# Attention: row maxima of the coming block over 16 key tiles instead of 17, VectorE's additions of probabilities one a step

## The reference, cut to what matters

```python
def one_block(qblk):
    s = jnp.einsum('bqkgd,blkd->bkgql', qblk, k).astype(jnp.float32) * scale
    p = jax.nn.softmax(s, axis=-1).astype(v.dtype)
    return jnp.einsum('bkgql,blkd->bqkgd', p, v)
```

## Time and profile before

| what | us |
|---|---|
| median of 3 runs | 3497.44 (3494.97 to 3501.01) |
| the profiled execution: its time | 3497.05 |
| the profiled execution: its span (first to last instruction) | 3495.4 |
| attention, from the first block to the last values | about 586 to 1818 |

### The profile page before, as it was taken

One profiled execution on the slowest core, in us unless ns is written; L12 is line 12 of the kernel. 1 busy time (PEld: TensorE's weight loads), 2 busy tenths in 40 slices (PEclk: granted clock), 3 DMA queues, 4 the chain that ended last, 5 costly groups with the idle time before them and its releaser, 6 DMA issues. The chain is left out here.

```text
span 3495.4 us, 39397 instructions
## 1 busy us (share of the span) xinstructions
PE 3276.0 (94%) x14481; PEld 2416.4 (69%) x14481; DVE 2103.9 (60%) x3047; ACT 1014.2 (29%) x1405; POOL 1272.1 (36%) x710
## 2 busy tenths in 40 slices
PE   6999766999999999999979979999999999999996
PEld 3888753655556565655647758888888888888885
DVE  3444435686777767677756655555555556665557
ACT  3232231343434434343433232222111111111111
POOL 1233201666666566555551122222222223332221
PEclk8999986999999999999999989999999999999998
DMA  5123296122321232232027861111111612221111
GB/s 228 55 87 90 74 344 176 43 63 52 99 58 52 53 88 57 52 75 49 16 64 256 290 234 66 48 48 48 48 48 48 247 60 72 72 72 55 48 47 48
DMA packets 221243, 325.91 MB, mean 93 GB/s; under 512 B 27152, under 2 KB 153488, under 8 KB 215824
## 3 DMA queue, kind: packets, MB, share of 16 engines
q1 hardware_dynamic: 201040, 295.14, 28.0%
q10 hardware_dynamic: 18944, 25.17, 2.2%
q0 software_dynamic: 1152, 4.19, 0.3%
HBM read 228.70 MB, written 95.75 MB: 93 GB/s over the span
## 5 line engine op out<-in xcount | busy, mean ns | idle before, releaser
L976 DVE TENSOR_REDUCE a_mpart<-a_mx 128x1 f32<-128x512 f32 (+1 forms) x960 | 592.8, 636 | 322.9 <-PE a_mx L1066 312.5
L921 POOL TENSOR_TENSOR a_acc_p<-a_acc_p,a_pf 128x1024 f32<-128x1024 f32 x240 | 581.1, 2421 | 233.3 <-ACT a_pf L957 211.6
L957 ACT ACTIVATE a_pf<-a_sc 128x1024 f32<-128x1024 f32 x432 | 441.7, 1025 | 468.7 <-PE a_sc L1091 467.8
L1623 DVE TENSOR_TENSOR f_yacc<-f_two,f_yacc 128x512 f32<-128x512 f32 x480 | 328.4, 690 | 257.7 <-PE f_two L1718 257.6
L1718 PE MATMUL f_two<-f_w_hi,f_h_hi 128*128 128x512 f32 x1024 | 398.4, 389 | 1.6 <-DVE f_h_lo L1636 1.6
L1718 PE MATMUL f_two<-f_w_hi,f_h_lo 128*128 128x512 f32 x1024 | 398.4, 389 | 0.0
L1718 PE MATMUL f_two<-f_w_lo,f_h_hi 128*128 128x512 f32 x1024 | 398.3, 389 | 0.0
L1104 PE MATMUL a_o<-a_pf,a_v 128*64 128x512 f32 x1728 | 390.5, 601 | 0.0
L1561 POOL TENSOR_TENSOR f_w_lo<-w_rows,f_w_hi 128x1024 fp32r<-128x1024 f32 x64 | 158.5, 2481 | 546.9 <-ACT f_w_hi L1520 546.7
L1633 DVE TENSOR_TENSOR f_relu<-f_relu 128x512 f32<-128x512 f32 x128 | 192.7, 1506 | 242.5 <-ACT f_relu L1530 242.5
L1104 PEld LDWEIGHTS a_o<-a_pf,a_v 128*64 128x64 f32 x1728 | 120.8, 138 | 231.0 <-issue 221.2
(11 more groups left out here) (266 smaller groups left out, 6074.5 us busy)
## 6 DMA issues: line engine op xcount, KB each, us to landing
w_rows<-in_w SPq DMA_DIRECT2D x128, 512.0 KB, 3.9
a_wa<-in_w_ada SPq DMA_DIRECT2D x6, 2048.0 KB, 9.8
ada_w<-in_w_ada SPq DMA_DIRECT2D x8, 1024.0 KB, 8.0
xt<-in_x_t SPq DMA_DIRECT2D x16, 512.0 KB, 3.6
o_m_hi<-s_mix ACTq DMA_DIRECT2D x8, 1024.0 KB, 7.1
o_m_lo<-s_mix ACTq DMA_DIRECT2D x8, 1024.0 KB, 9.4
o_x<-in_x ACTq DMA_DIRECT2D x16, 512.0 KB, 4.5
s_x<-o_x SPq DMA_DIRECT2D x16, 512.0 KB, 2.8
```

The lines of the kernel that those rows point to most:

```text
L921: nc.gpsimd.tensor_tensor(acc[:, :], left[:, :], pf[(b * KT + kt) % NPF][:, :], ALU.add).then_inc(added_p, 1)
L957: nc.scalar.activation(pf[n % NPF][:, :], sc[n % 2][:, :], ACT.Exp, scale=SCALES[0 if is_mla(b) else 1]).then_inc(exped, 1)
L976: nc.vector.reduce_max(mpart[:, s, k:k + 1], mx[c % 2][:, 0:CHUNKS[k][1]], AX.X).then_inc(mx_read, 1)
L1623: nc.vector.tensor_tensor(acc, two[:, o % 4, :], acc, ALU.add).then_inc(two_read, 1)
```

## The change

Three things change in `stage_attend`. `items_of` spreads the 40 items over steps 0 to 15, and steps 16 and 17 have none; three items now fall in steps 1, 3, 5, 7, 9, 11, 13 and 15. `columns` stands at the end of step 16 and not of step 17. VectorE's additions are issued one a step, each a step later than its tile: those of tiles 10, 11, 15 and 16 in steps 11, 12, 16 and 17, and that of tile 17 in step 0 of the next block, behind that step's reductions. GpSimd's work, the matmuls and their number, and the values are as before.

```diff
-        items_of = lambda kt: range(NI * kt // (KT - 1), NI * (kt + 1) // (KT - 1)) if kt < KT - 1 else range(0)
+        items_of = lambda kt: range(NI * kt // (KT - 2), NI * (kt + 1) // (KT - 2)) if kt < KT - 2 else range(0)
...
-                    if kt in (11, 17):
-                        if kt == 17 and b + 1 < NSB:
-                            columns(b + 1)
-                        for s in (kt - 2, kt - 1, kt):
-                            den_add(b, s)
+                    if kt == KT - 2 and b + 1 < NSB:
+                        columns(b + 1)
+                    if kt - 1 in DVE_STEPS:
+                        den_add(b, kt - 1)
+                    if kt == 0 and b:
+                        den_add(b - 1, KT - 1)
...
+            den_add(NSB - 1, KT - 1)
             normalise(NSB - 1)
             low(NSB - 1)
```

## The result

| | before | after |
|---|---|---|
| median of 5 runs, us | 3497.44 | 3562.21 |
| range | 3494.97 to 3501.01 | 3552.51 to 3565.65 |
| profiled execution | 3497.05 | 3552.51 |
| span | 3495.4 | 3550.8 |

The ratio after to before is 1.0176, 95% interval 1.0160 to 1.0192. The forecast of 3562 us met the median.

A forecast was written before the change was run, and what follows sets the result against it. TensorE was taken as the bound on average (busy 1205.81 of 1232 us), VectorE's reductions as setting the pace in GQA stretches. 54 us from stretches, 14 clock and -3 for L1009 made 65 on 3497.05: 3562 us, range 3528 to 3588.

The forecast's parts named there:

- GQA first stretch: First six score steps of a GQA block: tile 17's addition and 15 items for 14 add 1.4 us.
- GQA second: Second score stretch of a GQA block: no addition in it, 15 items against 14, +0.35 us.
- GQA third: Last GQA score stretch: tile 11's addition, and the write of the columns waiting for GpSimd's third addition, +0.8 us.
- MLA first: First score stretch of an MLA block: tile 17's addition delays item 4, and items are denser, +1.17 us.
- MLA third, with the copy: Last MLA score stretch in six blocks: +0.25 us, and +0.68 for the copy of step 12.
- row and values, nearly all of it the clock, in total: Lowered clock after TensorE's waits, at the row and inside stretches: more and longer waits cost +14 us.
- the signs named: Expected in the changed trace, among others: TensorE waits of 1 us or more at the item of steps 1 and 13.
- The copy: L1036 behind tile 11's addition in six MLA blocks: adds to the same stall, +0.68 us each.
- The rival with the early write: End of GQA third stretches: columns written ahead of GpSimd's third addition, total 3535 us; chance 0.22.
- The rival in which the clock falls at most of the waits: Row, stretch and copy waits: clock costs +40 us in place of +14, total 3590 or above; chance 0.11.
- L1009 in blocks 4 and 12: The 5.25 us multiplication's wait depends on how it meets GpSimd's chain; -5 to +10 us, taken as -3.
- Absorbed additions: Score stretches: VectorE's slack takes the additions, so only the early row counts, 21 us faster, 3476 us; chance 0.07.

The follow-up runs named there:

- e3_tile17: The kernel after, with tile 17's addition moved back to step 17, beside the values; 3543.13 us, 1.0132 of before.
- e4_tile11: The kernel after, with tile 11's addition moved back to step 11, beside the values; 3544.60 us, 1.0138 of before.
- e1_items: The kernel before, with only the items over 16 steps and the columns in step 16; additions stay grouped; 3527.53 us, 1.0094 of before.
- e5_after_neg: The kernel after without the write L985; the last reduction of columns negates and writes them itself; 3538.21 us, 1.0102 of before.
- e2_adds: The kernel before, with only the additions moved to one a step; items over 17 steps, columns in step 17; 3580.86 us, 1.0243 of before.
- e11_mid2: The kernel of e8_psum with four items as two pairs between the values of step 11, GQA blocks only; 3458.81 us, 0.9888 of before.
- e6_before_neg: The kernel before without the write L985; the last reduction of columns negates and writes them itself; 3479.39 us, 0.9936 of before.
- e8_psum: The kernel of e6_before_neg, with reciprocal and normalised output kept in PSUM, so L1009 and L1014 lack two SBUF inputs; 3470.91 us, 0.9915 of before.

## Why the prediction was right

The table has the working's terms beside the profile of after, in us a block but for its last three lines (eleven GQA blocks with items; eleven MLA blocks with a predecessor).

| term | forecast | measured |
|---|---|---|
| GQA first stretch | +1.4 | +1.61 |
| GQA second | +0.35 | +0.73 |
| GQA third | +0.8 | +0.80 |
| MLA first | +1.17 | +1.17 |
| MLA second, six blocks without copy | +0.35 | +0.37 |
| MLA third, with the copy | +0.93 | +0.95 |
| MLA third, the other six, sum | +3.5 | +3.6 |
| all stretches, in total | +54 - 3 | +57.2 |
| row and values, nearly all of it the clock, in total | +14 | -5.6 |

*The mechanism* stands step by step: five additions cost nothing before; two of them went to the head of a score stretch, and two banks don't cover 1.2 us. e3_tile17 and e4_tile11 show it for each alone. Of the signs named, the wait at the first late item is 1.12 us in GQA but only 0.64 in MLA.

*The split inside the terms was off,* and the sums hid it. By e1_items the items cost 0.70 us in the first GQA stretch and 0.48 in the first MLA one, where I had 0.1 to 0.2. By after less e3_tile17, tile 17's addition costs 0.92 and 0.68, where I had about 1.3 and 0.95. Two things were wrong in the count. It let an item that waited for its bank pass like any other, 0.233 us long and readable after 0.43; it holds TensorE 0.10 us longer, and is readable 0.10 later, and the denser spread has five such items in the first stretch where the old one had three (GQA) or two (MLA). The 0.07 us between a reduction's end and the matmul that waited for it was not the error: it is 0.054. And the term was the counted end of the stretch after (10.95) less the measured one before (9.53). Run through for the kernel before, the same count ends at about 9.2, so what it lacked stood on one side only. The second GQA stretch, where no addition hides it, has +0.73 for +0.35. The copy cost about 0.4 and not 0.68: its blocks' third stretch grew 1.12 from e1_items to after, the others' 0.75 (0.67 in blocks 17 and 21, whose row doesn't wait for GpSimd). In MLA the addition of tile 11 cost 0.67 for my 0.95.

*The write of the columns* came behind GpSimd's third addition, 1396.03 less 1385.22 = 10.81 into the stretch for my 10.85. The rival with the early write has no run for it, but e5_after_neg shows its price: 1.3 us a block. The rule of the Trainium skill (SBUF — State Buffer, "SBUF: two separate sides"), that of VectorE in a two-port mode and GpSimd the one that starts first keeps the ports for its whole instruction, gave the right result here. The trace agrees: the write of 2.12 us ends 0.03 behind GpSimd's addition. That the write, which has one SBUF input, runs in a two-port mode no row says; a reduction in its place takes 0.20 us in all 24 blocks of e5_after_neg.

*The clock.* My +14 was too large. In the profiled execution only block 3 fell. This is the first part of its values, against as long a part in block 14:

```profile
800.40:803.80 3.40, 3.40 (x12) 1.20 (x12) 1.52 (x2) 1.01 (x2) 0.00 (x0) 0.54 0.00 0
1397.00:1400.40 3.40, 3.40 (x19) 1.29 (x19) 1.41 (x2) 0.89 (x2) 0.00 (x0) 1.00 0.00 0
```

The other executions are slower at a lower mean clock: 3552.51 us at 0.968, 3556.98 at 0.967, 3563.39 at 0.966, 3562.21 and 3565.65 at 0.965. With two levels, 0.003 less means 0.006 of 3560 us more at the lower one and half of that lost, 10.7 us; the distance from the profiled execution to the median is 9.7. This is an estimate, since 0.001 of the clock is 3.6 us and no trace shows where those executions fell. On this reading the clock is -5.6 + 9.7 = +4 us at the median, for my +14. The stretches gave 57.2 for 51, and 3.9 us lie outside attention, for which I had nothing: 57.2 + 4 + 3.9 = 65. So the sum of 65 was met by luck: one term 10 us too large, two too small by as much.

The waits inside the stretches, which I had counted among the places, were not followed by a single fall: the clock is 1.00 in every score stretch of after from block 1 on. Behind the row the profiles show this, in GQA blocks: waits of 0.90 to 0.96 us and 4 falls in 11 (before); 1.13 to 1.19 and 1 and 4 in 11 (after, e3_tile17); 1.26 to 1.32 and 7 and 8 in 11 (e1_items, e4_tile11); 2.06 and 11 in 11 (e2_adds); no wait and none in 88 (the eight profiles from e5_after_neg on). So the waits are the cause, and long ones fall more often; why after has fewer falls than before I can't tell from these runs. The rival in which the clock falls at most of the waits is out.

*L1009 in blocks 4 and 12* lost its 5.25 us by the shift, as taken (-4.5 for -3). That was luck of phase: in e5_after_neg the two come back (5.6 us for the multiplication, second stretches 16.3).

*Absorbed additions*, the faster rival, fell: the idle time of VectorE that could take an addition lies beside the values. e11_mid2 used it where it lies.

3.9 of the 55.5 us between the two profiled executions lie outside attention, 2.9 of them in its later start (556.45 for 553.59). The edit does not touch that part, and the start differs as much between the other kernels (551.78 to 559.14).

## What to carry to other kernels

An engine's idle share says nothing about where its idle time lies. Before you spread grouped work evenly, look at what it stands beside: here five additions stood in front of matmuls that needed nothing from VectorE, and cost nothing. Where one engine follows another two buffers behind, an instruction put between costs much of its length: here 0.92 us (GQA) and 0.68 (MLA) for one of 1.22. And look first for short operations that wait for another engine: one small write less gave 20 us in the kernel before (e6_before_neg), and an input in PSUM for two more operations another 8.5 (e8_psum).

## What was new about the hardware

- VectorE's operations with two SBUF inputs, and the small write with one, waited for GpSimd instructions under way. What I hadn't expected is that they can lose to a whole row of them: 0.68 us became 9.96 behind six that followed without a gap (e2_adds), and 0.69 became 5.25 behind the last 0.12 us of one and three more before. With an input in PSUM the same operations took 0.70 and 0.68 us in all 24 blocks.
- A single 0.23 us matmul of the items put between the values' matmuls takes 0.43 us and makes the four before it 0.12 longer; a pair takes 0.66.
- A matmul of the items that had to wait for its bank started 0.054 us behind the end of the reduction, then held TensorE 0.10 us longer than one that hadn't waited, and its result was read 0.10 later (0.54 for 0.43).
